# Norms as columns of tokens, regrouped dense pieces in the heads, and a last attention that starts among its gate units

## The chip, the core and the metric

The kernel runs on one core of a Trainium2 chip. The metric is the device time of one execution in microseconds (us); lower is better. The core has five engines that matter here: TensorE (PE, with its weight loads shown as PEld), VectorE (DVE), ScalarE (ACT), GpSimd (POOL) and SyncE (SP, which issues most of the DMAs). Each engine works off its own queue in order, and they wait for each other by semaphores.

## What is computed

Two transformer blocks follow each other on 512 tokens of 1024 features (the second also has 256 context tokens). All is fp32 in and out.

```python
# first block
u = rms_norm(h, norm_mix_pre)
q, k, v ..., gate_a, gate_b = split(u @ w_in)
o_a = nsa_attention(...)            # compressed, selected and window keys, 8 heads
o_b = swa_sink_attention(...)       # window of 128, a sink per head, 8 heads
y = sigmoid(gate_a) * (o_a @ w_up_nsa) + sigmoid(gate_b) * (o_b @ w_up_swa)
h = h + rms_norm(y @ w_out, norm_mix_post)
f = square(relu(rms_norm(h, norm_mlp_pre) @ w_mlp_in)) @ w_mlp_out
h = h + rms_norm(f, norm_mlp_post)
# second block: layer 0 "A" (differential attention), layer 1 "B" (windowed attention)
for i in range(2):
    shift, scale, gate = split(silu(c) @ w_mod[i] + b_mod[i])     # and the same for the context
    hx = rms_norm(x, g[i]) * (1 + scale) + shift
    hc = rms_norm(ctx, g[i]) * (1 + scale_c) + shift_c
    x = x + gate * (mixer_i(hx, hc) @ w_o[i])
return rms_norm(x, final_g)
```

## The kernel before

**Layout.** Activations lie feature-major: 8 tiles of 128 features (partitions) by 512 tokens, or 768 with the context. A weight "unit" is a 1024x128 block of a matrix. SP loads it into `raw` (four buffers), ACT copies it to a rounded high part `w_h` (`split_high`, line 302), POOL subtracts to get the low part `w_l` (line 890), and PE makes three products for each of the 8 feature tiles: high by high, low by high, high by low (`products`, lines 317 and 321). A product of a unit with 512 tokens is thus 24 matmuls. Activations are split likewise: ACT writes the high tile, DVE the low tile.

**Norms.** Each RMS norm needs, for each token, the sum of squares over 1024 features, which lie on partitions. ACT squares the tiles into `sq` (two buffers), DVE adds most of them into `sqsum`, and PE multiplies with a 128x128 matrix of ones, so that each partition gets the sum of its token: a 128x512 result in PSUM. ACT then makes exp(-0.5 ln(mean + eps)) on 128x512 (`make_rstd`, lines 377 and 379) into the SBUF tile `rstd`, and DVE multiplies tiles by it. The norms are: `nm1` (input), `nm2a` (after w_out), `nm2b` (a sum for the next one), `nm3c` (context), `nm3a` (after the MLP), `nm3b` (before layer A), `nm4` (before layer B) and `nm5` (final).

**The order of the work.** It is written out by hand, engine by engine. The projections of the first block come first, then attention `A1` with the gate units woven in, w_up, w_out, and the MLP with 64 units, during which DVE also makes the modulation vectors from `w_mod` (`cps` holds the conditioning products in PSUM banks 4 to 7). Then come layer A's eight heads (`attend`), w_ao (its last feature tile apart, in `last_out`), the 20 units of layer B, attention `A2` of 16 steps, w_bo, and the final norm.

**Heads of layer A.** In `attend` PE alternates between the attention of one head (scores, `turns` that transpose probabilities, value products) and "dense" pieces of the next head's projections. A piece is one of the 8 feature tiles of a unit (6 matmuls of 512 and 256 tokens), and a head has 4 units (q, k, v, g), 32 pieces. A unit writes banks 0 and 1, and the next unit can start only when ACT has copied them out (`take`). The last head has no successor; its dense pieces are seven tiles of each of the eight w_ao units (`partial_out`, 56 pieces), whose results ACT copies to `ao_t` (`take_out`). The rotation of the next head's q and k (`rotate`) stands in DVE's queue at the fourth and fifth query tile.

**Layer B.** The units are 8 of q, 2 of k, 2 of v and 8 gates. The context tiles of the normed input are needed from unit 8 on; DVE and ACT make one of them in each of the units 0 to 7, beside the rotation of that unit's q. Behind unit 13 PE transposes v in two sets through banks 4 and 5. When all 20 units are done, a barrier (`end_phase("bqkv")`) stands ahead of `attn_pe`, `attn_act` and `attn_dve`. A step of `A2` has four rows of scores (two banks each, two slots), minima by DVE (line 615), exponentials by ACT (line 580), scaling by DVE (line 650), transposes by PE (line 516), a copy of each transposed block by ACT (line 564), and value products (line 527).

Of the kernel before, what the change touches and what calls it, by code (L numbers as in the profile page):

```python
# [11 lines left out]
P = 128  # L12
# [58 lines left out]
def build(nc, t, out):  # L71
# [3 lines left out]
    with ExitStack() as ctx:  # L75
# [53 lines left out]
        tick = sm(3)  # L129
        mulx = sm(32).rearrange("p (l v k) -> p l v k", l=2, v=2)  # L130
# [57 lines left out]
        epsh = at("epsh", z + 64, [P, S])  # L188
        varf = at("varf", z + 66, [P, S])
# [70 lines left out]
        PHASES = ["prep", "wout", "heads", "ao", "bqkv"]  # L260
# [76 lines left out]
        NORM_SEMS = ["src", "sq", "add", "mm", "ln", "r", "t", "hi", "lo"]  # L337

        class Norm:
# [4 lines left out]
            def __init__(self, **counts):  # L344
                self.base = dict(Norm.ends)
                for n in NORM_SEMS:
                    Norm.ends[n] += counts.get(n, 1 if n in ("mm", "ln", "r") else 8)
                self.src, self.sq, self.add, self.mm, self.ln, self.r, self.t, self.hi, self.lo = \
                    [Norm.sems[n] for n in NORM_SEMS]

# [30 lines left out]

        none = dict(src=0, t=0, hi=0, lo=0)
        nm1 = Norm(src=0, t=0)
        nm2a = Norm(**none, sq=0, add=KT + 1)
        nm2b = Norm(t=0, ln=0, r=0)
# [3 lines left out]
        nm4 = Norm(src=0, add=4)  # L389
        nm4c = Norm(src=0, sq=0, add=0, mm=0, ln=0, r=0)  # L390
        sq_odd = sem("sq_odd")
        nm5 = Norm(src=0, add=KT - 1, t=FIN, hi=0, lo=0)
# [71 lines left out]
        class Attn:  # L464
            def __init__(self, name, steps, slots, width, sbuf, ptbuf, sbn, finish):
# [9 lines left out]
                self.between_pe = self.between_act = self.between_dve = lambda eng, x: None  # L475
# [67 lines left out]
        def attn_pe(pe, A):  # L543
            attn_scores(pe, A, 0)
            attn_scores(pe, A, 1)
# [4 lines left out]
        def attn_act(act, A):  # L550
            def turned(n):
                st = A.steps[n]
                for b, (o, w) in enumerate(st["blocks"]):
                    x = A.blk[n] + b
                    act.wait_ge(A.t, x + 1)

                    if x >= 4:
                        need = x - 3
                        gd = sum(1 for s in range(len(A.steps)) if A.steps[s]["last"] and A.blk[s + 1] <= need)
                        if gd:  # L560
                            act.wait_ge(A.o, gd)
                        if need - gd:
                            act.wait_ge(A.k, need - gd)
                    nc.scalar.activation(A.pt[0:w, x % 4], ps[0:w, 4 + x % A.tb], ACT.Copy).then_inc(A.te, 1)
                    A.between_act(act, x)

            def finished(n):
                if A.steps[n]["last"]:
                    A.finish["act"](act, A, n, A.grp[n])

            for n, st in enumerate(A.steps):
                for r in range(REP):
                    m = n * REP + r
                    act.wait_ge(A.m, m + 1)
                    if st["sink"] is not None or st["clamp"]:
                        act.wait_ge(A.m, (n + 1) * REP)
                        act.wait_ge(mfix[A], fixn(A, n) + 1)
                    buf = A.sb[n % A.sbn][:, r, 0:st["keys"]]
                    c = (n % 2) * REP + r
                    nc.scalar.activation(buf, buf, ACT.Exp, bias=negm[:, c:c + 1], scale=-1.0,  # L580
                                         accum_out=sums[:, c:c + 1]).then_inc(A.e, 1)
                if st["sink"] is not None:
                    c = (n % 2) * REP
                    nc.scalar.activation(esk[:, c:c + REP], esk[:, c:c + REP], ACT.Exp).then_inc(A.e, 1)
# [1628 lines left out]
```

## Time and profile before

| what | value |
|---|---|
| median of 3 runs | 1720.45 us (1716.83 to 1722.75) |
| the profiled execution's own time | 1721.67 us |
| its span, first to last instruction | 1719.6 us |
| PE busy | 1588.1 us, 92% |
| PE weight loads busy | 1192.6 us, 69% |
| DVE busy | 936.6 us, 54% |
| ACT busy | 764.2 us, 44% |
| POOL busy | 494.5 us, 29% |
| mean granted clock of PE | 0.975 of full |

A busy share is the time in which an engine has an instruction in work, over the span. Weight loads overlap matmuls. The chain of work that ended last runs through PE for 73% of the span, through DVE for 14% and ACT for 6%. Times below are us from the span's start, and a number in brackets is the idle time of the engine ahead of the instruction, with what ended it.

### The profile page before, as it was taken

Reading aid. Unit: us, or ns where it says so; the run is one execution under the profiler, and the core shown is the slowest. Engines: PE = TensorE matmul, PEld = TensorE weight load, DVE = VectorE, ACT = ScalarE, POOL = GpSimd, SP = SyncE. Lnnn points to the kernel's source line nnn. Section 1 sums busy time; section 2 is a strip of 40 time slices with the busy share of each in tenths; the row PEclk is TensorE's granted clock in tenths of the full one; section 3 lists DMA queues with packets and bytes.
Section 4 is the critical chain, followed back from the end, with each engine's and each line's share of the span. In section 5 each row is a group of like instructions: output and inputs, shape, how many; then the busy total and the mean of one; then the engine's idle time right before and its main releaser. Section 6 shows DMA issues by size and latency. Waiting matters only on the chain.

```text
span 1719.6 us, 22679 instructions
## 1 busy us (share of the span) xinstructions
PE 1588.1 (92%) x7940; PEld 1192.6 (69%) x7940; DVE 936.6 (54%) x2204; ACT 764.2 (44%) x1411; POOL 494.5 (29%) x220
## 2 busy tenths in 40 slices
PE   7998999999899999998999999999989697979897
PEld 5885666677688888885777777677667477745455
DVE  7136555283788767556556444644471593156642
ACT  6227766524333222345335443554443531246653
POOL 4542232344244444442211111111224242310012
PEclk9999999999899999999999999999999899979999
DMA  6851112363466665431101111111111131210001
GB/s 193 175 140 45 61 57 73 115 224 115 146 196 193 197 188 195 156 98 62 50 31 44 38 37 37 37 37 37 37 38 50 37 90 59 77 34 1 1 13 62
DMA packets 48397, 149.28 MB, mean 87 GB/s; under 512 B 5782, under 2 KB 9110, under 8 KB 48184
## 3 DMA queue, kind: packets, MB, share of 16 engines
q1 hardware_dynamic: 37080, 112.45, 21.7%
q10 hardware_dynamic: 11232, 35.72, 6.4%
q8 instruction: 51, 0.84, 0.2%
q14 instruction: 34, 0.28, 0.1%
HBM read 141.53 MB, written 6.62 MB: 86 GB/s over the span
## 4 chain that ended last, share of the span: by engine, by line
PE 73%; DVE 14%; ACT 6%; issue 4%; DMA 1%; POOL 0%; ACTq 0%; DVEq 0%; SPq 0%
PE ps L317 37%; PE ps L321 18%; PE ps L497 3%; PE ps L1192 3%; PE ps L516 3%; PE ps L527 3%; PE ps L1228 2%; DVE b_sb L615 1%; DVE x2l L1806 1%; ACT sb L580 1%; DVE xn L1800 1%; PE ps L1204 1%; PE ps L971 1%; DVE ropea L1932 1%; ACT w_h L302 1%
## 5 line engine op out<-in xcount | busy, mean ns | idle before, releaser
L890 POOL TENSOR_TENSOR w_l<-raw,w_h 128x1024 fp32r<-128x1024 f32 (+1 forms) x190 | 457.1, 2406 | 993.8 <-ACT w_h L302 993.8
L302 ACT ACTIVATE w_h<-raw 128x1024 fp32r<-128x1024 f32 x190 | 200.8, 1058 | 396.6 <-PE ps L317 330.6
L317 PE MATMUL ps<-x2h,w_h 128*128 128x512 f32 (+1 forms) x816 | 248.5, 370 | 46.1 <-DVE x2l L1806 22.6
L317 PE MATMUL ps<-x1h,w_h 128*128 128x512 f32 x584 | 239.0, 409 | 19.9 <-POOL w_l L890 10.3
L317 PE MATMUL ps<-x2h,w_l 128*128 128x512 f32 (+1 forms) x816 | 232.0, 350 | 0.0
L321 PE MATMUL ps<-x2l,w_h 128*128 128x512 f32 (+1 forms) x816 | 231.8, 349 | 0.0
L317 PE MATMUL ps<-x1h,w_l 128*128 128x512 f32 x584 | 231.4, 396 | 0.0
L321 PE MATMUL ps<-x1l,w_h 128*128 128x512 f32 x584 | 230.8, 395 | 0.0
L317 PEld LDWEIGHTS ps<-x2h,w_h 128*128 128x128 f32 x816 | 132.3, 190 | 95.1 <-issue 56.1
L317 PEld LDWEIGHTS ps<-x2h,w_l 128*128 128x128 f32 x816 | 132.1, 191 | 20.7
L321 PEld LDWEIGHTS ps<-x2l,w_h 128*128 128x128 f32 x816 | 132.4, 191 | 19.9 <-issue 0.2
L317 PEld LDWEIGHTS ps<-x1h,w_h 128*128 128x128 f32 x584 | 111.8, 191 | 46.1 <-issue 10.4
L317 PEld LDWEIGHTS ps<-x1h,w_l 128*128 128x128 f32 x584 | 111.6, 191 | 24.4
L321 PEld LDWEIGHTS ps<-x1l,w_h 128*128 128x128 f32 x584 | 112.0, 192 | 20.6 <-issue 0.2
L1865 DVE CUSTOM_DVE_ANT_0 terms<-mraw,ps 128x1024 f32<-128x1024 f32 x96 | 116.8, 1217 | 2.5
L1982 DVE CUSTOM_DVE_ANT_0 a_p<-ps,small 128x768 f32<-128x768 f32 (+1 forms) x96 | 71.3, 776 | 68.8 <-issue 68.8
L317 PE MATMUL ps<-m_h,w_h 128*128 128x512 f32 x256 | 99.6, 389 | 0.0
L321 PE MATMUL ps<-m_l,w_h 128*128 128x512 f32 x256 | 99.6, 389 | 0.0
L317 PE MATMUL ps<-m_h,w_l 128*128 128x512 f32 x256 | 99.6, 389 | 0.0
L1490 ACT ACTIVATE a_p<-a_p,small 128x768 f32<-128x768 f32 (+1 forms) x96 | 75.1, 785 | 24.4 <-DVE small L1982 24.4
L615 DVE CUSTOM_DVE_ANT_0 b_sb<-ps,bm 128x512 f32<-128x512 f32 (+1 forms) x64 | 45.9, 755 | 40.0 <-PE ps L497 39.9
L897 POOL TENSOR_TENSOR g_stage<-g_stage,rstd 128x512 f32<-128x512 f32 x16 | 20.5, 1281 | 148.9 <-ACT g_stage L784 148.9
(310 smaller groups left out, 2490.6 us busy)
## 6 DMA issues: line engine op xcount, KB each, us to landing
raw<-in_w_mlp SPq DMA_DIRECT2D x64, 512.0 KB, 4.2
mraw<-in_w_mod ACTq DMA_DIRECT2D x51, 512.0 KB, 3.8
raw<-in_w_a SPq DMA_DIRECT2D x32, 512.0 KB, 3.5
raw<-in_w_att SPq DMA_DIRECT2D x25, 512.0 KB, 11.2
raw<-in_w_b SPq DMA_DIRECT2D x20, 512.0 KB, 3.5
raw<-in_w_g SPq DMA_DIRECT2D x16, 512.0 KB, 3.6
raw<-in_w_ao SPq DMA_DIRECT2D x9, 512.0 KB, 3.5
gates<-g_stage ACTq DMA_DIRECT2D x16, 256.0 KB, 2.1
```

Source lines behind the costliest of these rows:

```text
L302: nc.scalar.activation(split(u)[0], raw[:, u % RAW], ACT.Copy).then_inc(w_hi, 1)
L317: mm = nc.tensor.matmul(o, w[:, k], xh(k), start=(first and k == k0 and wi == 0), stop=(last and k == k1 - 1 and wi == 1))
L321: mm = nc.tensor.matmul(o, w[:, k], xl(k), start=False, stop=False)
L497: mm = nc.tensor.matmul(A.sbank(m + h)[:, o:o + rhs.shape[-1]], st["q"](r + h), rhs, start=st["kstart"][c], stop=True, skip_group_check=True)
L516: mm = nc.tensor.transpose(ps[0:w, 4 + x % A.tb, y * P:(y + 1) * P], A.sb[n % A.sbn][:, r, o:o + w], ident[:])
L527: mm = nc.tensor.matmul(ps[h * HD:(h + 1) * HD, 6 + g % 2, cols], st["v"](h)[b], A.pt[0:w, x % 4, h * 2 * P:(h + 1) * 2 * P], start=(st["f ...
L615: nc.vector.tensor_tensor_reduce(out=A.sb[n % A.sbn][:, r, 0:st["keys"]], in0=A.sbank(m)[:, st["off"]:st["off"] + st["keys"]], in1=st["bia ...
L890: nc.gpsimd.tensor_tensor(l[:, ks], raw[:, u % RAW, ks], h[:, ks].bitcast(F32), ALU.subtract).then_inc(w_lo, 1)
L1192: mm = nc.tensor.matmul(pair(1 + 2 * m)[:, o:o + n], aq[ms, qt * P:(qt + 1) * P], ak[ms, key:key + n], start=True, stop=True)
L1490: nc.scalar.activation(buf, buf, ACT.Exp, bias=negm[:, cc:cc + 1], scale=-1.0, accum_out=sums[:, cc:cc + 1]).then_inc(ha["e"], 1)
L1865: nc.vector.tensor_tensor_reduce(out=terms[:], in0=mraw[:, c % MRAW].rearrange("p k m -> p (k m)"), in1=cps[:, w, :], scale=0.5, scalar=0. ...
L1982: nc.vector.tensor_tensor_reduce(out=a_p[qt % 3][m][:, 0:n], in0=pair(1 + 2 * m)[:, 0:n], in1=zero.to_broadcast([P, n]), scale=1.0, scalar ...
```

## The change

It has three parts, named in its title.

**Norms.** For `nm2a`, `nm2b`, `nm3c`, `nm3a`, `nm3b`, `nm4` and `nm5` the sum of squares is made with the squares as the stationary operand and one column of ones as the moving one, so that a block of 128 tokens gives one column: 128x4 for 512 tokens, 128x6 for 768 (`column_sums`). ACT takes a square root of that (`root`), DVE a reciprocal (`invert`), and PE spreads each column over 128 partitions by a matmul of the broadcast column with the identity (`spread`), into a PSUM bank that DVE's multiplications then read in place of `rstd`. A tiny Sqrt activation stands some time ahead of three of the norms. The final norm is spread twice, and ACT copies one of these for POOL's two tiles. `nm1` and the norm inside the heads stay as they were.

```diff
+        def column_sums(src, bank, n, first, last):
+            for b in range(n // P):
+                mm = nc.tensor.matmul(ps[:, bank, b:b + 1], src[:, b * P:(b + 1) * P], ones[:, 0:1],
+                                      start=(first and b == 0), stop=(last and b == n // P - 1))
+            return mm
+        def root(act, nm, bank, n):
+            nm.wait(act, "mm", 1)
+            nc.scalar.activation(dev[:, 0:n // P], ps[:, bank, 0:n // P], ACT.Sqrt, bias=eps_t[:], scale=1.0 / D).then_inc(nm.ln, 1)
+        def invert(v, nm, n):
+            nm.wait(v, "ln", 1)
+            nc.vector.reciprocal(rcol[:, 0:n // P], dev[:, 0:n // P]).then_inc(nm.rc, 1)
+        def spread(bank, b0, b1):
+            for b in range(b0, b1):
+                mm = nc.tensor.matmul(ps[:, bank, (b - b0) * P:(b - b0 + 1) * P], rcol[:, b:b + 1].to_broadcast([P, P]), ident[:],
+                                      start=True, stop=True)
+            return mm
...
             nm3a.wait(pe, "sq", KT)
-            nc.tensor.matmul(ps[:, 4], ones[:], sq[:, 1, 0:S], start=False, stop=True).then_inc(nm3a.mm, 1)
+            column_sums(sq[:, 1], 4, S, False, True).then_inc(nm3a.mm, 1)
+            nm3a.wait(pe, "rc", 1)
+            nm3c.wait(pe, "lo", KT)
+            spread(5, 0, 4).then_inc(nm3a.r, 1)
```

In `last_out` the squares of every tile go to PE two tiles later, and DVE no longer adds any of them:

```diff
-                    if m >= 2 and m % 2 == 0:
-                        nm4.wait(pe, "sq", m)
-                        sum_part(sq[:, 1], m == 2, False).then_inc(sq_odd, 1)
-                nm4.wait(pe, "add", N_OUT // 2)
-                sum_part(sqsum, False, False)
+                    if m >= 2:
+                        nm4.wait(pe, "sq", m - 1)
+                        column_sums(sq[:, m % 2], 6, SC, m == 2, False).then_inc(sq_sum, 1)
+                nm4.wait(pe, "sq", N_OUT - 1)
+                column_sums(sq[:, 0], 6, SC, False, False)
                 nm4.wait(pe, "sq", N_OUT)
-                sum_part(sq[:, 1], False, True).then_inc(nm4.mm, 1)
+                column_sums(sq[:, 1], 6, SC, False, True).then_inc(nm4.mm, 1)
+                nm4.wait(pe, "rc", 1)
+                spread(7, 0, 4).then_inc(nm4.r, 1)
+                spread(5, 4, 6).then_inc(nm4c.r, 1)
```

Behind the w_out norm DVE's three operations per tile are reordered so that the first low tile comes one operation earlier, and the conditioning products `cps` are cut in two: one half inside the w_out units, one behind the last low tile.

**Heads.** The sizes of the dense pieces change, and DVE's rotations of the next head's q and k come behind the loop over query tiles:

```diff
                 scores(1)
-                dense(4 if more else 3)
+                dense(4)
...
                 turns(4)
-                dense(2 if more else 4)
+                dense(4)
...
-                dense(2 if more else 3)
+                if not more:
+                    dense(3)
                 turns(5)
-                dense(2 if more else 1)
+                if more:
+                    dense(4)
...
-                dense(6 if more else 7)
+                dense(4 if more else 7)
...
-                    if qt in (3, 4) and more:
-                        rotate((i, c + 1), qt - 3, "qk"[qt - 3])
+                if more:
+                    rotate((i, c + 1), 0, "q")
+                    rotate((i, c + 1), 1, "k")
```

**Layer B.** The context tiles are made two per unit in units 0 to 3. The second set of v transposes uses banks 6 and 7. The last gates write banks 6 and 7 (`gate_bank`), the barrier ahead of `A2` is gone, and the scores of the steps 0 and 1 stand between the halves of the last two gate units. ACT and DVE have the parts of these steps between their parts of the gates, and in every step of `A2` ACT copies the first two transposed blocks of the step before among its four exponentials:

```diff
+            pe.wait_ge(hb["free"], 16)
+            for n, u in enumerate((N_B - 2, N_B - 1)):
+                attn_scores(pe, A2, n, (0, 1))
+                split_ready(pe, U_B + u)
+                pe.wait_ge(hb["free"], u - 1)
+                products(U_B + u, b_parts(u), 0, KT // 2, last=False)
+                attn_scores(pe, A2, n, (2, 3))
+                products(U_B + u, b_parts(u), KT // 2, KT, first=False).then_inc(unit, 1)
...
+            for u in range(N_B - 2):
+                take_b(u)
+            attn_exps(act, A2, 0)
+            take_b(N_B - 2)
...
+                act.wait_ge(A.m, m + 1)
+                if n and A.slots == 2 and r >= 2:
+                    attn_turned(act, A, n - 1, (r - 2,))
...
+            attn_minima(v, A2, 0, (0, 1))
+            gate_b(N_B - 3)
+            attn_minima(v, A2, 0, (2, 3))
+            attn_minima(v, A2, 1, (0, 1))
+            gate_b(N_B - 2)
+            attn_scale(v, A2, 0)
+            attn_minima(v, A2, 1, (2, 3))
```

The gate of unit 19 is taken behind step 1 on ACT and DVE. `A1` keeps its order.

## Rows read from the trace of the kernel before

**Rows 1.** The page: its first line, and two groups of its fifth section.

```profile
span 1719.6 us, 22679 instructions
...
L890 POOL TENSOR_TENSOR w_l<-raw,w_h 128x1024 fp32r<-128x1024 f32 (+1 forms) x190 | 457.1, 2406 | 993.8 <-ACT w_h L302 993.8
...
L615 DVE CUSTOM_DVE_ANT_0 b_sb<-ps,bm 128x512 f32<-128x512 f32 (+1 forms) x64 | 45.9, 755 | 40.0 <-PE ps L497 39.9
```

**Rows 2.** Waits of PE: line, whom for, us in total, times, longest.

```profile
PE ps L317 <- DVE x2l L1806: 22.6, 7, 8.6
PE ps L497 <- DVE small L615: 16.1, 19, 1.6
...
PE ps L317 <- ACT ao_t L1478: 6.5, 6, 1.2
PE ps L317 <- ACT a_vT L1459: 5.4, 7, 0.8
PE ps L1204 <- DVE a_p L1997: 5.2, 7, 0.8
```

**Rows 3.** Busy time by window: stretch, length, engines, granted clock, DMA.

```profile
1427.00:1433.00 6.00, 5.63 (x24) 4.89 (x25) 0.22 (x1) 0.00 (x0) 0.00 (x0) 0.70 0.00 0
```

**Rows 4.** Nearest prices: timeline, then lines of PEld and of DVE.

```profile
181.27 0.63 PE L497 MATMUL ps<-kcmp,q_n 64*128 64x32 f32 x8
...
1538.18 1.09 PE L516 MATMUL ps<-ident,b_sb 128*128 128x128 f32 x8
...
L497 PEld LDWEIGHTS ps<-kcmp,q_n 64*128 64x128 f32 x64 | 4.5, 193 | 3.2 <-issue 2.7 <-DVE small L615 0.4
...
L643 DVE RECIPROCAL small<-small 128x4 f32<-128x4 f32 x48 | 8.6, 180 | 1.6
```

**Rows 5.** Timeline of PE, ACT and DVE at the w_out norm.

```profile
426.40 1.12 PE L1034 MATMUL ps<-sq,ones 128*128 128x512 f32 x2 [0.85 <-ACT sq L1357]
...
428.85 1.28 ACT L379 ACT_TABLE_LOAD   x1
...
431.11 1.42 DVE L1780 SCALAR_TENSOR_TENSOR f_t<-f_t,small,rstd 128x512 f32<-128x512 f32 x2 [0.46 <-DVEq L265]
```

**Rows 6.** Timeline of PE and DVE at the two norms behind the MLP.

```profile
794.23 1.12 PE L1070 MATMUL ps<-sq,ones 128*128 128x512 f32 x2 [0.72 <-ACT sq L357]
...
802.90 9.57 PE L1088 MATMUL ps<-sq,ones 128*128 128x512 f32 x16 [1.79 <-ACT sq L1430]
...
800.17 1.42 DVE L1896 SCALAR_TENSOR_TENSOR f_t<-f_t,small,rstd 128x512 f32<-128x512 f32 x2 [4.00 <-ACT rstd L1425]
...
815.17 1.41 DVE L1800 SCALAR_TENSOR_TENSOR xn<-hc,small,rstd 128x512 f32<-128x512 f32 x2 [4.80 <-ACT rstd L1434]
```

**Rows 7.** Timeline of PE in the heads: a value product, eight score instructions.

```profile
1112.60 5.31 PE L1228 MATMUL ps<-a_pt,a_v 128*128 128x512 f32 x12
...
1274.22 1.56 PE L1192 MATMUL ps<-a_k,a_q 64*128 64x512 f32 x8
```

**Rows 8.** Timeline of PE and DVE around the end of w_ao.

```profile
1349.51 1.13 PE L1143 MATMUL ps<-sq,ones 128*128 128x512 f32 x2 [1.05 <-ACT sq L1557]
...
1354.22 1.13 PE L1143 MATMUL ps<-sq,ones 128*128 128x512 f32 x2 [1.07 <-ACT sq L1557]
...
1358.92 2.07 PE L1143 MATMUL ps<-sqsum,ones 128*128 128x512 f32 x2 [2.10 <-DVE sqsum L2049]
...
1367.97 1.41 DVE L1800 SCALAR_TENSOR_TENSOR xn<-hc,small,rstd 128x512 f32<-128x512 f32 x2 [9.10 <-ACT rstd L379]
```

**Rows 9.** Timeline of PE at the waits inside the b units.

```profile
1427.37 0.98 PE L317 MATMUL ps<-x2h,w_h 128*128 128x512 f32 x2 [8.62 <-DVE x2l L1806]
...
1476.60 0.87 PE L1269 MATMUL ps<-ident,b_vT 128*128 128x128 f32 x6 [2.65 <-DVE b_v L2079]
```

**Rows 10.** Timeline of ACT and PE where the last attention starts.

```profile
1499.39 1.06 ACT L302 ACTIVATE w_h<-raw 128x1024 fp32r<-128x1024 f32 x1 [3.90 <-PE ps L317]
...
1529.08 1.97 PE L516 MATMUL ps<-ident,b_sb 128*128 128x128 f32 x8
```

More of the change, by code:

```diff
@@ L548, in attn_pe, with attn_turned @@
                 attn_out(pe, A, n)
[L550 to L565, printed above, removed]
+        def attn_turned(act, A, n, bs):
+            st = A.steps[n]
+            for b in bs:
+                o, w = st["blocks"][b]
+                x = A.blk[n] + b
+                act.wait_ge(A.t, x + 1)
+                if x >= 4:
+                    need = x - 3
+                    gd = sum(1 for s in range(len(A.steps)) if A.steps[s]["last"] and A.blk[s + 1] <= need)
+                    if gd:
+                        act.wait_ge(A.o, gd)
+                    if need - gd:
+                        act.wait_ge(A.k, need - gd)
+                nc.scalar.activation(A.pt[0:w, x % 4], ps[0:w, 4 + x % A.tb], ACT.Copy).then_inc(A.te, 1)
+                A.between_act(act, x)
@@ L569, in finished @@
                     A.finish["act"](act, A, n, A.grp[n])
[L571 to L584, printed above, removed]
-                else:
-                    act.wait_ge(A.e, 5 * n + 4)
-                    nc.scalar.activation(spare, eps_t[:], ACT.Copy).then_inc(A.e, 1)
+            for n in range(n0, len(A.steps)):
+                attn_exps(act, A, n)
                 if n:
-                    turned(n - 1)
+                    attn_turned(act, A, n - 1, range(2 if A.slots == 2 else 0, len(A.steps[n - 1]["blocks"])))
                 if n >= 2:
                     finished(n - 2)
-            turned(len(A.steps) - 1)
+                A.after_act(act, n)
+            attn_turned(act, A, len(A.steps) - 1, range(len(A.steps[-1]["blocks"])))
             finished(len(A.steps) - 2)
@@ L1087, in _ @@
                 nm3b.wait(pe, "sq", k + 1)
-                mm = nc.tensor.matmul(ps[:, 6], ones[:], sq[:, k % 2, 0:S], start=(k == 0), stop=(k == KT - 1))
-                mm.then_inc(n3_sum, 1)
+                column_sums(sq[:, k % 2], 6, S, k == 0, k == KT - 1).then_inc(n3_sum, 1)
+            nm3b.wait(pe, "rc", 1)
+            spread(7, 0, 4).then_inc(nm3b.r, 1)
             for k in range(KT + LAG):
@@ L1139, in partial_out @@
                         mm.then_inc(unit, 1)
-            def sum_part(src, first, last):
-                nc.tensor.matmul(ps[:, 6, :], ones[:], src[:, 0:S], start=first, stop=last)
-                return nc.tensor.matmul(ps[:, 7, 0:C], ones[:], src[:, S:SC], start=first, stop=last)
             def last_out():
@@ L1285, in _ @@
             nm5.wait(pe, "add", KT - 1)
[L1286 removed]
+            column_sums(sqsum, 4, S, True, False)
             nm5.wait(pe, "sq", KT)
[L1288 removed]
+            column_sums(sq[:, 1], 4, S, False, True).then_inc(nm5.mm, 1)
+            nm5.wait(pe, "rc", 1)
+            spread(5, 0, 4).then_inc(nm5.r, 1)
+            spread(6, 0, 4).then_inc(nm5.r, 1)
         @block.scalar
@@ L1422, in _ @@
             act.wait_ge(varf_ok, 1)
-            nc.scalar.activation(rstd[:, 0:S], varf[:], ACT.Ln).then_inc(nm3a.ln, 1)
-            nm3a.wait(act, "ln", 1)
-            nc.scalar.activation(rstd[:, 0:S], rstd[:, 0:S], ACT.Exp, scale=-0.5).then_inc(nm3a.r, 1)
+            nc.scalar.activation(dev[:, 0:4], varc, ACT.Sqrt).then_inc(nm3a.ln, 1)
             for k in range(KT):
```

347 lines of the change are left out of this document (198 added, 149 removed).

## The prediction

> **What bounds the kernel now.** I began with the page: a span of 1719.6 us [rows 1]. The execution it shows took 1721.67 us, so 2.1 us lie around the span, and it is 1.2 us above the median of 1720.45. TensorE (PE) is busy over nine tenths of the span, so only what PE waits for, what it does at half clock, or work taken from it can shorten the kernel. The second view was who keeps PE waiting [rows 2]: low tiles of normed activations, the minima of the attentions, and evacuations that come when PE has just finished a unit and wants its bank back. I then read the timeline where the diff touches these waits. PE also pays after long gaps: after the 8.62 us gap at 1418.75 the clock stood at 0.70 on average over 6 us, a mix of 1.2 and 2.4 GHz [rows 3].
>
> **Prices.** The column sums and the spreads do not exist before. A column sum of 512 tokens is 4 fp32 matmuls with one moving column, 8 pairs of weight load and matmul. The nearest row is 8 pairs with 32 moving columns: 0.63 us in all. I take 0.63 (0.95 for the 12 pairs of 768 tokens), and near twice that where the clock is halved; above, 8 loads that overlap nothing, at 0.19 each, are 1.5. A spread of 4 blocks is 8 pairs with 128 columns, which is what 8 transposing pairs cost: 1.09 us. A spread at 1.2 GHz would cost what the first such step does, 1.97. A reciprocal on 128x4 is 0.18 us, and I take the same for a 128x4 activation [rows 4, 10]. I allow 0.1 us for each hand-over.
>
> What the old chain holds is seen behind the w_out product [rows 5]: from the last ones-matmul (426.40) to the first user (431.11) 4.7 us, with Ln, Exp and a 1.28 us table load ahead of each. The new chain is sum 0.63, root 0.3, reciprocal 0.3, spread 1.3, hand-over and barrier 0.4, so 2.9 to 3.0: it saves 1.7 (0.8 with the halved clock, 2.0 above). Here the root's table is loaded under the w_out products, where ScalarE has room; half of the conditioning products go there too, and the other half behind the last low tile, where they delay ScalarE's first split of the MLP by nothing that I can see (its cover gone, at most 0.5).
>
> ScalarE's table loads were weighed against the skill. The trace loads a table for Ln and again for Exp, 1.28 us each. The Trainium skill (ScalarE: Activation LUTs, Table sets: the hidden batching unit) says Ln and then Exp need one load, and Exp and then Sqrt two; by that rule the old norm would be a load cheaper than the trace shows, and this edit would save 1.3 us less per norm. The trace disagrees, and the sum goes by it.
>
> **Part by part.**
> 1. w_out norm: 1.7, as above.
> 2. The two norms behind the MLP [rows 6]. The first chain ran from 794.23 to 800.17. Now it is 2.8 us and ends near 797.0, but PE waits for it, and the 6.3 us of context products that it did meanwhile (to 801.11, the end before the 1.79 us wait) now run to 803.3. The sums of squares then start later than before (802.90), but they no longer trail: a square of 0.63 us and a column sum of 0.5 alternate in two buffers at 0.65 us per tile, and end near 808.5 in place of 812.47. The second chain takes 1.9 in place of 2.7 us. Gain 4.3 (3.0 halved, 5.0 if sums cost nothing).
> 3. Seven head turns with a successor. Two waits stand in each [rows 2]: 0.74 us for a combined probability tile, since VectorE rotates the next q before it, and 0.77 for the evacuation of v, since PE reaches the end of that unit just then. The rotations now come after the last tile, where VectorE is idle; and the end of the v unit falls ahead of the value product, 5.3 us [rows 7]. Both waits go, 1.5 x 7 = 10.5. It costs nothing while those covers hold; if others surface, half, 5; 11.5 above.
> 4. The last head. Six waits of 1.1 us for ao_t [rows 2] are each at a unit's end inside a dense piece. Pieces now end with the unit, so scores (1.56 us for eight instructions, half for four) or turns stand there [rows 7]. The first gains nothing, because the seventh product must now wait for its low tile ahead of the scores; the next four give 1.2, 0.6, 0.6 and 0.6. Gain 3 (1.5 to 4.5).
> 5. The w_ao tail and its norm [rows 8]. Two tiles take 4.7 us from sum to sum, with a 1.05 us wait for a fresh square. With sums two tiles late nobody waits, and PE needs 2 x 1.1 for products (4.7 less the wait and 1.3 of sums) and 2 x 0.65 for sums, 3.5; over three and a half pairs 4.2. From the last product (1356.82) to the first user (1367.97) it was 11.15 us. Now: 2.1 for update, split and square as before, 0.65 sum, 0.3 root, 0.3 reciprocal, 12 spread pairs 1.7, barrier 0.4, so 5.5. Together 9.9; this stretch is sparse and may run at half clock, so I take 9 (7 to 10.5).
> 6. The eighth b unit [rows 9]. PE waits 8.62 us for the eighth context tile, which VectorE makes one per unit. At two per unit all eight are there after four units, some 15 us before they are wanted. 8.62 goes, and so does the slow clock behind it (6 us at 0.70, 1.8): 10.4 (8.6 to 10.8). The second set of v transposes has its own banks: 2.65 goes (2.0 to 2.7).
> 7. The start of the last attention [rows 10]. From the end of unit 17 (1499.39) to the first transposes (1529.08) it is 29.7 us: 10.9 of two units, then scores and softmax alone, at half clock. Now the scores lie among the units. PE's work is 10.9 + 5 x 1.1 = 16.4, but VectorE's chain is longer: four minima at 0.75 each [rows 1], four exponentials about as long, the gate of unit 18 (queued behind them on ScalarE with its 1.06 us split), scaling behind GpSimd's 2.4 us low tile [rows 1], and two more minima before the third step's scores. Walked through, transposes start 19.1 us after unit 17. Gain 10.6. Later the gate of unit 19 and its split sit between exponentials (-1.5), and the second step is at full clock (+1.4). I take 10.5 (7 to 13). Queued behind gate 18 on VectorE are the scale of step 0 and half the minima of step 1; PE waits for these with its second half unit as cover.
> 8. ScalarE copies turned blocks between exponentials. In most steps PE waits for minima and not for these, so they buy little: 2 over 16 steps (0 to 4).
> 9. The end. Norm chain 1.7 shorter for VectorE's six outputs, but GpSimd's two get theirs from a second spread and a copy, 0.8 earlier; the last transfer leaves some 1.3 earlier (0.7 to 1.75). The chain's old parts are those of part 1 [rows 5].
>
> Sum: 1.7 + 4.3 + 10.5 + 3 + 9 + 10.4 + 2.65 + 10.5 + 2 + 1.3 = 55.4. From 1721.7 that is 1666; I say 1666 us for the median.
>
> **Rivals.**
> - Weight loads pace the column sums. For: each load is shown with 0.19 us. Against: 8 pairs in 0.63 [rows 4] means that they overlap. If nothing did, a tile of part 5 would take 3.4 us, and the eight sums of part 2 12 us: together some 20 us back, 1686. The Trainium skill (TensorE: Matmul & The Clock Gate, LDWEIGHTS (loading the stationary operand)) gives columns / 1.2 ns, 107 ns for each of these loads; by that 12 pairs are 1.3 us, parts 2 and 5 lose about 7 us, and the time is 1673. The trace disagrees where 8 loads of 128 columns fit into 0.63. A mechanism of this kernel with that price, 1673 to 1686, gets 0.08.
> - The early attention does not pay: the chain over gate 18 is as long as the old idle time, or the gates' splits collide with every step. Then part 7 is 3 and not 10.5, 1674. For: two engines' queues are threaded through each other, and GpSimd's low tile holds up VectorE's scaling. 0.17.
> - The heads stay at their period, since VectorE's and ScalarE's chain and not PE's is the pace: part 3 gives 0 to 3, 1675. Against: in a turn only these two waits are above 0.4 us, and PE is busy in nearly all the rest. 0.09.
> - The table of the root lacks a function used between roots, so that it is loaded again in each norm: 5 x 1.28 back, 1672. For it speaks only that Ln and Exp did so. 0.06.
> - The other side: in the last attention the third and fourth exponential now wait for transposes of the step before, which wait for scaled probabilities. If that closes a circle, each of 16 steps (9.1 us for the first, from 1529.08 to 1538.18 [rows 4, 10]) grows. From 3.5 us per step on the kernel is slower: 1730 at 4 us. Against: transposes of two blocks are there when two exponentials are done. 0.02.
> - The change does little, since other waits take over in most places: 1710 to 1722, 0.03.
>
> **How the numbers follow.** The forecast of 1666 has a chance of 0.55. Its terms' lower ends add up to 39, their upper ends to 65, but they seldom fall together. The range runs from 1656 to 1682 and takes in the single rivals at 1672 to 1675. Within 0.3% (about what a measurement of this kernel can tell from no change) lies almost nothing: faster 0.95, same 0.02, slower 0.03.
>
> **What would show it.** Right: no wait of PE for x2l longer than about 4 us behind the w_ao norm, none near the eighth b unit; 8 column pairs near 0.6 us; one table load or none per norm, outside the chain; no wait of PE for a_vT or a_p above 0.5 us in the heads, so that a turn is 1.5 us shorter; 19 us from unit 17 to the first transposes of the last attention. Wrong: PE waits for VectorE's minima among the last units, table loads right ahead of roots, column sums above 1 us, steps of the last attention longer than now, or new waits at the unit boundaries of the heads.

## The result and the profile after

The changed kernel takes 1689.98 us (median of four, 1689.45 to 1696.08) against 1719.94 for the kernel before: a ratio of 0.9834, with a 95% interval of 0.9806 to 0.9863. It is 30 us faster. The forecast was 1666 us, 54 faster by the same median, with a range that ended at 1682. So the sign was right, the size was a little over half, and the time lies outside the range.

The page of the changed kernel, its first line and the two groups that answer to [rows 1]:

```profile
span 1688.6 us, 23139 instructions
...
L928 POOL TENSOR_TENSOR w_l<-raw,w_h 128x1024 fp32r<-128x1024 f32 (+1 forms) x190 | 454.8, 2395 | 970.5 <-ACT w_h L304 970.5
...
L640 DVE CUSTOM_DVE_ANT_0 b_sb<-ps,bm 128x512 f32<-128x512 f32 (+1 forms) x64 | 45.9, 755 | 37.4 <-PE ps L521 37.2
```

The waits of PE, which answer to [rows 2]:

```profile
PE ps L521 <- DVE small L640: 11.6, 17, 1.5
...
PE ps L319 <- DVE x2l L1897: 8.5, 10, 2.6
PE ps L319 <- DVE x1l L1868: 6.4, 7, 3.5
...
PE ps L319 <- DVE a_g L2035: 2.9, 1, 2.9
...
PE ps L319 <- ACT ao_t L1537: 2.2, 3, 1.0
```

By this view the change did nearly all that it should: the waits for x2l in the norms of layers A and B fell from 22.6 to 8.5 us, those for a_vT and for a_p have left the list, ao_t has 2.2 in place of 6.5. By the two pages PE is idle for 82.9 us of the span and not 131.5 (span less busy time). That is 48.6 us less waiting for a span that is 31.0 us shorter: PE is also busy for longer, 1605.7 us and not 1588.1. Cutting both spans at the same events shows where. All rows are lengths in us, of which the column "after, less before" adds up to the 31.0 us between the spans; e2 is an experiment below.

| stretch (ends at) | before | after | after, less before | forecast | e2, less before |
|---|---|---|---|---|---|
| start to PE's wait for w_out's last square | 425.55 | 425.08 | -0.5 | 0 | -0.4 |
| w_out norm and MLP (wait for its last square) | 367.97 | 369.31 | +1.3 | -1.7 | +1.5 |
| two norms (first a product with x2l) | 24.00 | 27.46 | +3.5 | -4.3 | -1.4 |
| first a units, seven turns (last head's scores) | 426.16 | 415.71 | -10.5 | -10.5 | -12.5 |
| last head (wait for the last ao_t) | 95.31 | 90.84 | -4.5 | -3.0 | -4.7 |
| last pass of w_ao (its last product) | 17.83 | 24.50 | +6.7 | -9.0 with the next | -0.6 |
| norm of w_ao (first b product) | 13.59 | 13.57 | 0.0 | | -4.9 |
| b units (end of unit 17) | 128.98 | 117.08 | -11.9 | -13.05 | -11.9 |
| start of the last attention (first transposes) | 29.69 | 17.84 | -11.9 | -10.5 with the second step | -11.8 |
| its steps and the last product | 176.51 | 173.16 | -3.4 | -2.0 | -3.4 |
| end | 14.01 | 14.05 | 0.0 | -1.3 | +0.8 |

Everything that moves work between other work came out near its forecast, from 1.1 us less (the b units) to 1.5 us more. Everything that has to do with a norm did not: 11.5 us are lost in the four rows from the w_out norm to that of w_ao (without the heads), where 15.0 of gain were forecast, and the end gives nothing for 1.3. The seven turns hit 10.5 partly by luck, as is told below. The timeline of PE in the changed kernel, at the norms behind the MLP and in the last pass of w_ao, which answers to [rows 6, 8]:

```profile
793.44 0.95 PE L387 MATMUL ps<-ones,sqsum 128*128 128x1 f32 x8
...
805.37 11.45 PE L387 MATMUL ps<-ones,sq 128*128 128x1 f32 x64
...
1333.42 1.39 PE L387 MATMUL ps<-ones,sq 128*128 128x1 f32 x12
...
1347.58 0.84 PE L1200 MATMUL ps<-x2h,w_l 128*128 128x512 f32 x2
1348.22 2.55 PE L387 MATMUL ps<-ones,sq 128*128 128x1 f32 x12
...
1352.70 7.67 PE L387 MATMUL ps<-ones,sq 128*128 128x1 f32 x36
1360.95 2.93 PE L402 MATMUL ps<-ident,small 128*128 128x128 f32 x12 [0.58 <-DVE small L397]
```

Two things are to be seen. A column sum of 8 pairs takes 0.95 us and one of 12 takes 1.39, not 0.63 and 0.95. And a few microseconds later the same sum takes 2.55, and even the products beside it take 0.84, where the same two products took 0.51 in the kernel before:

```profile
1356.31 0.51 PE L1156 MATMUL ps<-x2h,w_l 128*128 128x512 f32 x2
```

The windows of the changed kernel say why; the column behind POOL's is the granted clock:

```profile
803.00:806.00 3.00, 3.00 (x29) 3.00 (x27) 3.00 (x6) 0.00 (x0) 0.00 (x0) 1.00 0.02 5
806.00:809.00 3.00, 3.00 (x23) 3.00 (x24) 2.91 (x5) 1.88 (x3) 0.00 (x0) 0.81 0.00 0
809.00:815.00 6.00, 6.00 (x30) 6.00 (x30) 0.00 (x0) 1.91 (x4) 0.00 (x0) 0.50 0.00 0
...
1333.00:1336.00 3.00, 3.00 (x25) 2.83 (x23) 1.42 (x3) 1.79 (x3) 0.76 (x1) 1.00 0.37 66
1336.00:1342.00 6.00, 6.00 (x30) 5.71 (x31) 2.28 (x4) 0.94 (x2) 0.00 (x0) 0.58 0.13 55
1342.00:1348.00 6.00, 6.00 (x23) 5.43 (x23) 1.14 (x2) 1.60 (x2) 0.00 (x0) 0.50 0.00 0
```

PE is shown as busy all the time, 6.00 of 6.00 us, and its clock is nevertheless granted at 0.50, that is 1.2 in place of 2.4 GHz. It was doing one-column sums just before: weight loads with one column streamed behind each. In the kernel before, where PE was less busy, the clock was at 1.00 in the same stretches:

```profile
809.00:815.00 6.00, 3.19 (x7) 0.97 (x6) 1.37 (x3) 5.17 (x7) 0.00 (x0) 1.00 0.00 0
1342.00:1348.00 6.00, 5.18 (x25) 3.68 (x24) 4.41 (x8) 2.54 (x3) 2.37 (x2) 1.00 0.29 87
```

At 0.50 a tile of the last pass takes 4.48 us (1343.74 to 1348.22 from sum to sum), where the prediction had 3.5 us for two.

A last surprise stands at head 0. The Sqrt table is in ScalarE when the gate's Tanh comes:

```profile
855.75 1.28 ACT L1520 ACT_TABLE_LOAD   x1
857.04 0.81 ACT L1520 ACTIVATE a_g<-ps 128x768 f32<-128x768 f32 x1
```

PE waits 2.94 us for a_g there (at 858.98), and 1.51 in the kernel before, which loads no table ahead of this gate:

```profile
853.26 0.59 PE L317 MATMUL ps<-x2h,w_h 128*128 128x512 f32 x2 [1.51 <-DVE a_g L1940]
```

### The profile page after: what moved, and what is told of

Same layout as the page of the kernel before. It is cut to its first block, busy times and chain, and to the rows that moved or that the text cites. A ratio compares the mean times of both kernels' runs of the same rounds, so it can differ in the third digit from the quotient of the medians.

```text
span 1688.6 us, 23139 instructions
## 1 busy us (share of the span) xinstructions
PE 1605.7 (95%) x8164; PEld 1229.9 (73%) x8164; DVE 936.9 (55%) x2206; ACT 750.5 (44%) x1401; POOL 491.7 (29%) x220
## 4 chain that ended last, share of the span: by engine, by line
PE 81%; DVE 9%; ACT 5%; issue 4%; POOL 1%; DMA 0%; PEldq 0%; ACTq 0%; POOLq 0%; PEld 0%; DVEq 0%
PE ps L319 41%; PE ps L323 20%; PE ps L521 3%; PE ps L1239 3%; PE ps L540 3%; PE ps L551 3%; PE ps L1275 2%; PE ps L387 2%; DVE b_sb L640 2%; PE ps L1251 1%; PE ps L1009 1%; ACT sb L601 1%; DVE tg L1824 1%; ACT w_h L304 1%; DVE b_sb L675 1%
## 5 line engine op out<-in xcount | busy, mean ns | idle before, releaser
L319 PE MATMUL ps<-x1h,w_h 128*128 128x512 f32 x584 | 239.9, 411 | 17.2 <-POOL w_l L928 10.4
```

The lines of the kernel that those rows point to most:

```text
L319: mm = nc.tensor.matmul(o, w[:, k], xh(k), start=(first and k == k0 and wi == 0), stop=(last and k == k1 - 1 and wi == 1))
```

## Experiments

My theory after this comparison (A): the one-column sums cost both by themselves and by the clock that they bring down. The main rival (B): the new chain of root, reciprocal and spread, with its hand-overs over three engines, costs more than Ln and Exp did.

**e1: the squares of w_ao added on VectorE.** Two column sums in place of eight.

```diff
-                    if m >= 2:
-                        nm4.wait(pe, "sq", m - 1)
-                        column_sums(sq[:, m % 2], 6, SC, m == 2, False).then_inc(sq_sum, 1)
-                nm4.wait(pe, "sq", N_OUT - 1)
-                column_sums(sq[:, 0], 6, SC, False, False)
+                nm4.wait(pe, "add", N_OUT - 1)
+                column_sums(sqsum, 6, SC, True, False)
...
+                if m:
+                    add_square(v, nm4, m - 1, SC)
```

> The changed kernel, but in the last pass of w_ao VectorE adds up the squares (128x768 adds, about 0.95 us each by the trace of before) and TensorE makes two column sums at the end and not eight. Theory A (the one-column sums are what costs: eight of them at 1.4 to 2.55 us, and they drag the granted clock of their stretch to 0.50): a tile then takes VectorE's 1.14 + 0.95 = 2.1 us in place of 4.48, and from the last wait for ao_t (1329.74 in the changed kernel) to the first b products it is 27 to 29 us and not 36.7; 8 to 9.5 us faster than the changed kernel, 1681 to 1682. Theory B (the chain behind the sums, root, reciprocal and spread over three engines, is what costs): the chain is untouched, so under 3 us are gained, 1687 to 1690.

Measured: 1682.57 us. From 1329.37 to the first b product at 1356.73 it is 27.4 us, 9.4 less than in the changed kernel, as A had it; the median is 7.4 less. But the clock still fell, this time where PE waited for an add. Timeline and windows of e1:

```profile
1345.36 2.72 PE L387 MATMUL ps<-ones,sqsum 128*128 128x1 f32 x12 [3.39 <-DVE sqsum L367]
...
1335.00:1341.00 6.00, 4.20 (x19) 2.93 (x20) 6.00 (x10) 2.79 (x4) 0.00 (x0) 1.00 0.19 73
...
1344.00:1350.00 6.00, 4.64 (x22) 4.64 (x22) 1.31 (x3) 1.19 (x2) 3.09 (x1) 0.50 0.21 55
```

**e2: 64 columns in place of one.** The same sums, and 63 columns of each block that nobody reads.

```diff
-                mm = nc.tensor.matmul(ps[:, bank, b:b + 1], src[:, b * P:(b + 1) * P], ones[:, 0:1],
+                mm = nc.tensor.matmul(ps[:, bank, b * 64:(b + 1) * 64], src[:, b * P:(b + 1) * P], ones[:, 0:64],
...
-            nc.scalar.activation(dev[:, 0:n // P], ps[:, bank, 0:n // P], ACT.Sqrt, ...
+            nc.scalar.activation(dev[:, 0:n // P], ps[:, bank, 0:n // P * 64:64], ACT.Sqrt, ...
```

> The changed kernel, but each column sum moves 64 columns of ones per block and not one, so TensorE streams 64 times the columns behind the same weight loads; the extra columns are not read. Theory A1 (what halves the clock is that TensorE hardly streams columns while it makes these sums): the granted clock of the last pass of w_ao and of the sums behind the MLP stays near 1.00, a sum of 768 tokens stays near 1.4 us, and 8 to 14 us come back, 1676 to 1682. Theory A2 (weight loads alone set the pace and the clock has another cause, such as the waits of the stretch): the clock falls as before and the time is 1689 to 1695, a little more for the columns.

Measured: 1671.53 us (ratio to the kernel before 0.9716, 0.969 to 0.9741), 18.5 us faster than the changed kernel by an edit that only adds work to PE, and more than the 8 to 14 us that I expected. Timeline and windows of e2 at the same two places:

```profile
805.55 7.55 PE L387 MATMUL ps<-ones,sq 128*128 128x64 f32 x64
...
1333.76 1.45 PE L387 MATMUL ps<-ones,sq 128*128 128x64 f32 x12
...
1338.56 4.13 PE L387 MATMUL ps<-ones,sq 128*128 128x64 f32 x36
1343.27 1.60 PE L402 MATMUL ps<-ident,small 128*128 128x128 f32 x12 [0.58 <-DVE small L397]
...
809.00:815.00 6.00, 5.26 (x43) 4.89 (x42) 0.32 (x3) 2.32 (x5) 0.00 (x0) 1.00 0.00 0
...
1335.00:1341.00 6.00, 6.00 (x49) 5.73 (x48) 2.39 (x5) 3.59 (x4) 1.02 (x1) 1.00 0.01 3
```

Twelve pairs take 1.45 us with 64 columns and 1.39 with one: at full clock the columns are nearly free. The clock stays at 1.00 in these two stretches, so the 36 last pairs take 4.13 and not 7.67 us and the spread 1.60 and not 2.93. This settles A's second half, since the edit changes nothing there but how many columns PE streams. It is not a lucky execution either: in all eight traced kernels with 64 columns and eight sums (e2 and e5 to e11) the last pass of w_ao takes 17.1 to 17.2 us and the norm behind it 8.7, and with one column the same pass takes 24.5 in the changed kernel and 17.8 in e3, and the norm 13.6 in both. Of the 18.3 us between the two spans 17.0 lie in the two norms, the last pass and its norm; most of the rest is in the seven turns (2.0), where the clock is at 0.50 from 859 to 862.5 behind the wait for a_g in the changed kernel, and at 1.00 behind the same wait in e2.

**e3: the sums behind the MLP among context products.** `first_ctx(1)` is cut into pieces that stand behind the single sums.

```diff
-            first_ctx(1)
             for k in range(KT):
                 nm3b.wait(pe, "sq", k + 1)
                 column_sums(sq[:, k % 2], 6, S, k == 0, k == KT - 1).then_inc(n3_sum, 1)
+                if k < KT - 1:
+                    first_ctx(1, k, k + 1 if k < KT - 2 else KT)
```

> The changed kernel, but behind the MLP the eight column sums of the second norm stand between the products of the second context unit and not behind both. Theory A (few columns, low clock, and a chain that starts too late): the sums run at full clock at 0.95 to 1.05 us, the last ends near 813 and not 816.8, the spread takes 1.1 and not 2.1 us; 4 to 5 us faster than the changed kernel, 1685 to 1686. Rival (the squares' own pace, one in 1.26 us from VectorE, is the bound): about 1 us, 1689.

Measured: 1683.87 us (1681.73 to 1690.74), which looks like a hit and isn't one. In its own stretch (from 794.41 to 820.48) it gained 0.6 us, because the clock fell there all the same, to 0.73 at 806 and 0.50 from 809 on. Another 6.7 us are in the last pass of w_ao, which the edit does not touch: there the clock held until 1343.3 and not until 1337, although e3 was only 1.4 us ahead, so that three more sums ran at 1.40 us. Windows of e3:

```profile
809.00:815.00 6.00, 6.00 (x30) 6.00 (x29) 0.00 (x0) 0.63 (x1) 0.00 (x0) 0.50 0.00 0
1335.00:1341.00 6.00, 6.00 (x47) 5.67 (x47) 3.04 (x6) 1.99 (x3) 0.00 (x0) 1.00 0.05 20
...
1344.00:1350.00 6.00, 6.00 (x30) 5.90 (x29) 1.14 (x2) 1.90 (x2) 2.35 (x1) 0.50 0.10 10
```

The place where the clock gives way is not fixed in such a stretch; a total of a few microseconds less proves nothing about an edit without its window.

**e4: the second norm behind the MLP and that of w_ao wholly as before**, in the changed kernel: `column_sums` there replaced by the ones-matmuls into 128x512 (and 128x256), VectorE's adds of every other square, `make_rstd` in place of `root`, `invert` and `spread`.

> The changed kernel with the second norm behind the MLP and the norm of w_ao wholly as before: wide ones-matmuls, pairs of squares added on VectorE, Ln and Exp with two table loads each. By the stages of the two traces these norms cost 3.5 and 6.6 us more than before, so theory A gives 1690 - 10 = 1680 us, and another 1.4 less where the Exp table is there again for the gate of head 0 (1678.6). The rival, that the new norms gain as forecast and the loss comes from elsewhere (clock or buffers of the stages ahead), gives over 1692.

Measured: 1674.62 us. Undoing what the change's title begins with makes the kernel 15 us faster, 5 more than the stages gave, since the clock that stays at 1.00 (0.50 only from 1346 on, in the wait behind the last sums) helps the neighbours too. From the end of the last sum of w_ao's norm to the first b product it is 5.69 us in e4, 6.10 in the changed kernel and 4.75 in e2. So the new chain is 0.9 us shorter than the old one at full clock, and 0.4 longer at half clock, where its spread takes 2.93 us and not 1.60. B is wrong: what the chain costs too much is again the clock. Against e2, which keeps it, e4 is 3.1 us slower, although it has no Tanh table to load at head 0.

The next six runs stand on e2, whose clock is steady in the two stretches of sums.

**e5 and e6: the two edits of the heads.** e5 puts VectorE's two rotations back between the combinations; e6 puts back TensorE's pieces.

```diff
e5
                         mins(qt + 2)
-                if more:
-                    rotate((i, c + 1), 0, "q")
-                    rotate((i, c + 1), 1, "k")
+                    if qt in (3, 4) and more:
+                        rotate((i, c + 1), qt - 3, "qk"[qt - 3])
e6
-                dense(4)
+                dense(2 if more else 4)
...
-                dense(4 if more else 7)
+                dense(6 if more else 7)
```

> The kernel of e2 (64-column sums, 1671.5 us, granted clock steady in the two norm stretches), with VectorE's rotations of the next q and k back between the combinations of the probability tiles, as before the change. If the rotations are what made TensorE wait 0.74 us for a combined tile in each turn, the seven turns are 0.74 us longer each: 5.2 us, 1676.7. Rival (TensorE's new pieces alone would have removed that wait): within 1 us of e2.

> The kernel of e2 with TensorE's dense pieces in the heads and in the last head cut as before the change (two and six tiles around the value products, not four and four; three and one in the last head). By the trace the wait of 0.77 us for a_vT returns in seven turns, 5.4 us, and the waits for ao_t in the last head, about 3 (forecast) to 4.5 us (measured): 1679.9 to 1681.4 in all. Rival (the pieces do nothing once the rotations are moved): within 1 us of e2 but for the last head, 1674.

Measured: 1677.98 and 1681.71 us, 6.4 and 10.2 us over e2. The waits of PE, of e5 and then of e6:

```profile
PE ps L1251 <- DVE a_p L2092: 5.2, 7, 0.9
```

```profile
PE ps L319 <- ACT ao_t L1535: 6.5, 6, 1.2
PE ps L319 <- ACT a_vT L1516: 5.4, 7, 0.8
```

Each part of the change removes exactly the wait that it was said to, and each alone leaves the other. A turn is 55.00 us in e5, 55.07 in e6, 54.01 in e2 (54.08 in the changed kernel) and 55.97 before. Undoing them costs 0.99 and 1.06, about the whole 1.96, and more than the 0.74 and 0.77 of the waits; where the other 0.5 us of a turn come from is not shown. The last head is 93.72 us in e6 and 90.62 in e2, so the pieces are worth 3.1 there.

**e7: ScalarE's copies of turned blocks behind all four exponentials.**

```diff
-                if n and A.slots == 2 and r >= 2:
-                    attn_turned(act, A, n - 1, (r - 2,))
```

> The kernel of e2 with ScalarE's copies of turned blocks in the last attention again behind all four exponentials of the next step. Forecast in the prediction: 2 us over 16 steps (0 to 4), so 1673.5 (1671.5 to 1675.5). Rival: they pace the steps, and more than 4 us come back, over 1675.5.

Measured: 1675.68 us, 4.2 over e2. Its trace is 2.5 us longer from the last attention's third step to the last product, with waits of PE for b_pt of 3.4 us in nine places where e2 has 1.0 in two. The trace agrees with the forecast of 2 within its range, while the medians' 4.2 lie just above it, on the side of the rival; whether the other 1.7 us are more than the spread of the runs (1674.69 to 1676.54, and 1667.46 to 1672.49 for e2) stays open.

**e8: the last attention begun behind the last gate.** Units 18 and 19 go back into the loop of units, and scores, exponentials and minima of step 0 and 1 behind it; the gates keep their new banks, and no barrier is put back.

> The kernel of e2 with the last attention begun behind the last gate and not among the gates, its copies still between exponentials; gates keep their own banks. The traces give 11.85 us from the end of unit 17 to the first transposes (forecast 10.5), so 1682 to 1684. Rival (the early start only moves a wait, since the steps are paced by VectorE and ScalarE): under 6 us, below 1677.5.

Measured: 1682.39 us (1677.93 to 1687.46), 10.9 over e2. In the trace it is 11.0 us more from the first b product to the first transposes and nothing in the steps behind them (173.18 us and 173.16), so the rival of a wait that is only moved is out. PE waits again for the gate and for each pair of minima:

```profile
PE ps L521 <- DVE small L640: 16.4, 20, 1.6
...
PE ps L521 <- DVE b_g L2139: 2.4, 1, 2.4
```

**e9: the Tanh table ahead.** One activation of one column right behind the root, while ScalarE waits for the spread.

```diff
             nc.scalar.activation(dev[:, 0:4], ps[:, 6, 0:256:64], ACT.Sqrt, ...).then_inc(nm3b.ln, 1)
+            nc.scalar.activation(dev[:, 6:7], eps_t, ACT.Tanh)
```

> The kernel of e2 with one more activation: a Tanh of one column right behind the root of the second norm behind the MLP, so that its table is loaded while ScalarE waits for the spread. If the load of 1.28 us ahead of head 0's gate is what lengthened TensorE's wait for a_g from 1.51 to 2.94 us, the wait is 1.5 us again and 1.4 us come back, 1670.1. Rival (the gate is late for another reason, or the table is put out again before the gate): the wait stays at 2.9 us, 1671.5.

Measured: 1669.8 us (1668.85 to 1672.66), 1.7 under e2; by the total alone it can't be told from e2. In the trace the load stands right behind the root (811.44), and PE's wait is what it was before the change:

```profile
PE ps L319 <- DVE a_g L2036: 1.5, 1, 1.5
```

**e10: VectorE's order behind the w_out norm as before.** A low tile two tiles behind its scale.

```diff
-            for k in range(KT):
-                if k >= 1 and k + 1 < KT:
-                    f_scale(k + 1)
-                if k + 1 < KT and k >= 1:
-                    f_add(k + 1)
-                f_low(k)
...
+            for k in range(KT + 2):
+                if k < KT:
+                    f_scale(k)
+                if 1 <= k <= KT:
+                    f_add(k - 1)
+                if k >= 2:
+                    f_low(k - 2)
```

> The kernel of e2 with VectorE's order behind the w_out norm as before the change (a scale, an add and a low tile two tiles apart). Theory: VectorE is the pace from the first low tile to the eighth, 2.05 us a tile in the new order, because each low tile waits for ScalarE's split of the same tile, and 1.93 in the old; the new order has its first low tile a step earlier (about 1.3 us) and loses it again over eight tiles. So the first tile comes 1.2 us later and the eighth 0.5 to 1 us earlier, and the time is 1670.5 to 1671.5. Rival: TensorE at half clock is the pace, and the later start costs 1 us, 1672.5.

Measured: 1671.1 us; by the total it can't be told from e2. The trace tells it. The first low tile comes at 432.71 (e2: 431.45), most tiles are 1.92 us apart (e2: 2.05), and the seventh starts at 443.59 (e2: 444.34), although e10 is 0.3 us later at its first scale. Not all of these 2.0 us is the distance of the tiles: the new order also has 2.66 us between its first two, and the old one only 1.26 between its sixth and seventh, when no scale is left. And the 0.13 us a tile are no wait for ScalarE's split, which my expectation named as the cause: VectorE goes from a scale to the add behind it in 0.78 us in e2, where that add needs this scale, and in 0.65 in e10. From the wait for w_out's last square to that for the MLP's it is 367.5 us, 1.9 less than in e2 and 0.5 less than before the change. Timeline of PE in e10:

```profile
433.60 0.77 PE L319 MATMUL ps<-x1h,w_h 128*128 128x512 f32 x1 [4.42 <-DVE x1l L1868]
```

**e11: e2 with the edits of e9 and e10.**

> The kernel of e2 with the edits of e9 and e10 together: if they add, 2 us less than e2, 1669.5.

Measured: 1668.63 us (1667.36 to 1668.88), ratio 0.97 (0.9682 to 0.9718), 21 us faster than the changed kernel and the lowest median of all runs, though its 2.9 us under e2 are within the spread of e2's runs (1667.46 to 1672.49).

**e12: e11, with every other square of w_ao added on VectorE**, so that six sums of 64 columns are left.

> The kernel of e11, and in the last pass of w_ao VectorE adds every other square (as before the change), so TensorE makes six 64-column sums and not eight: per two tiles TensorE has 2.2 us of products and 1.45 of sum, 3.65 and not 4.8. The last product comes 3.3 us earlier, but the last sums wait 2.1 us for an add, as in the trace of before. Net 1 to 2 us less than e11, 1667.5 to 1668.5, as long as the granted clock stays at 1.00. If the clock falls in the sparser stretch the sums cost 2.5 us and the kernel is slower than e11, 1671 or more.

Measured: 1671.85 us (1671.39 to 1673.39), 3.2 over e11: the expectation's second branch. Two sums fewer, and from the first product of the last pass (1317.94) to the first b product it takes 5.7 us longer than in e11. Timeline and windows of e12:

```profile
1336.68 2.82 PE L387 MATMUL ps<-ones,sqsum 128*128 128x64 f32 x12 [2.10 <-DVE sqsum L2144]
...
1332.00:1335.00 3.00, 2.57 (x18) 2.15 (x18) 1.28 (x3) 1.15 (x2) 0.00 (x0) 1.00 0.00 0
1335.00:1338.00 3.00, 1.32 (x6) 1.33 (x7) 1.62 (x3) 1.59 (x2) 2.17 (x1) 0.70 0.00 0
1338.00:1344.00 6.00, 5.42 (x26) 5.23 (x26) 0.19 (x1) 0.27 (x1) 0.83 (x1) 0.50 0.29 87
```

In e11 the clock is at 1.00 from 1326 to 1338. Its extra sums fill PE's waits, and at the end of the stretch that is worth more than what they cost.

## Why the prediction was wrong, step by step

**The price of a column sum** is the step that failed first. I took 0.63 us for 8 pairs, from score instructions with 32 moving columns [rows 4]. Their name shows a stationary operand of 64 rows, 64x128, and in the kernel they alternate between two heads, which lie in the lower and the upper 64 partitions. The row was used for sums of 128 rows as if neither mattered; which of the two makes it cheap no run separates. A row with 128x128 operands stood beside it, 8 transposing pairs in 1.09 us, and I used it for the spreads only. Measured at full clock: 0.95 us for 8 pairs, 1.39 for 12, so 0.12 us a pair. Part 2 even took 0.5 us for its sums of 8 pairs, and part 5 took 0.65 for its own, which have 12 pairs each. I had given "weight loads pace the column sums" 0.08, and argued it away by that same row. The Trainium skill (TensorE: Matmul & The Clock Gate, LDWEIGHTS (loading the stationary operand)) has 107 ns for each load of 128 columns. By that 12 loads are 1.28 us, an estimate; the trace comes near it with 1.39 us for 12 pairs, and what I called the trace's disagreement was my choice of row.

**The clock** is the larger one. Part 5 says "this stretch is sparse and may run at half clock, so I take 9 (7 to 10.5)", and parts 1 and 2 have the halved clock only in a lower end. The clock at 0.50 is no mark-down of a microsecond: it nearly doubles every sum (1.39 to 2.55), slows the products between them (0.51 to 0.84) and doubles the spread (1.60 to 2.93). I had looked for low clock behind gaps, as in [rows 3]. Here PE is shown busy without a gap when the clock falls. e2 puts a number on it: with the clock held in the stretches of sums and nothing else improved, 18.5 of the 24 us that were missing are there. Of my rivals only those in which the change does little or harm lay at 1690 or above. The one that came true, that weight loads pace the sums, was priced without the clock and ended at 1686. The range was also too narrow by its own terms: their lower ends add up to 35.6 us and not to 39, which alone allows 1686.

**Part 1** (1.7, came out as a loss of 1.3): the chain itself gained 1.6, from 4.71 us (426.40 to 431.11) to 3.12 (426.01 to 429.13), and the first low tile reaches PE at 432.29 in place of 435.20. It was given back in part by something that I did not cost at all, the new order of VectorE's three operations a tile. e10 puts 1.9 us on it. Even with the old order only 0.5 of the 1.6 is left at the end of the stretch; where the rest goes stays open.

**Part 2** (4.3, came out as a loss of 3.5): both clock and pair price. In e2 the stretch gains 1.4. Of the 2.9 us that are missing there, 2.4 are the eight sums, 7.55 us where 5.2 were forecast, and 0.8 the context products ahead of them, 7.1 us where 6.3 were: behind the first norm's chain the clock is at 0.50 under them (799 to 801), in e2 as in the changed kernel, and 64 columns did not help there. PE had just waited twice, 0.74 and 0.86 us; in the kernel before it did these products in place of waiting.

**Parts 3 and 4** (10.5 and 3): right in mechanism, 1.89 us a turn for 1.5, 4.5 for the last head. e5 and e6 show that the two waits are separate and add up. That part 3 came out at 10.5 to the tenth is luck: seven turns of 1.89 are 13.2, and 2.7 of it were lost again in the same stretch. Half of that is the Tanh table, 1.4 us at head 0, which part 3 lacks. I had given "the table of the root lacks a function used between roots" 0.06 and priced it inside the norms; the load came outside them, once, in front of a gate. e9 shows it.

**Part 5** (9, came out as a loss of 6.7): as above. With the clock held, in e2, it gains 5.5 (4.9 and 0.6); the rest is about what eight sums of 1.39 us cost over the 0.95 of my price list.

**Part 6** (13.05): 11.9. The eighth tile is in time and the second set of transposes does not wait, as said. The difference lies at the start of the units: from the second low tile on PE now waits 1.7 us in four places and 0.56 once for a weight's low part, where it waited 0.96 in two before (the eighth tile's 8.62 aside).

**Parts 7 and 8** (10.5 and 2): 11.85 and 3.35. Walked through, the start was to take 19.1 us and took 17.84. e8 and e7 give 10.9 and 4.2 when undone, and 11.0 and 2.5 by the trace.

**Part 9** (1.3): nothing. The new chain from the last product to VectorE's first output is 6.07 us where it was 6.10: two sums of 1.05 and 1.03 are as long as the wide ones (1.13 and 1.02), and two spreads, at a falling clock, take 3.56 us together. The price came from part 1, where the old chain took 4.71 us from the last ones-matmul to the first user. Here it took only 3.69 (1708.00 to 1711.69), since the first table load lies under the sums. ACT in the kernel before:

```profile
1707.68 1.28 ACT L1591 ACT_TABLE_LOAD   x1
...
1709.77 1.28 ACT L1593 ACT_TABLE_LOAD   x1
```

The new chain takes 3.71 (1676.91 to 1680.62) and not 3.0. What root and reciprocal save on the one load that is left goes into the spread.

## What to carry to other kernels

A matmul with one moving column cost here what its pair of load and matmul takes, 0.12 us, and a string of them also cost TensorE's clock. When the clock falls in a stretch where the engine looks busy, try more columns in the same instructions (e2) before taking instructions away (e12); products put between the sums did not hold it (e3). Price an instruction by a row whose stationary operand has the same rows and columns and lies in the same partitions, and where the clock may fall price everything in the stretch at both levels, neighbours included. And read a gain of a few microseconds off the stretch that was edited, for the clock can give or take as much elsewhere.

## What was not expected of the hardware

- TensorE at 6.00 us busy of 6.00 by the profile is granted 0.50 of its clock while it runs one-column sums, and 1.00 with the same sums of 64 columns; at full clock these cost 0.06 us more for 12 pairs.
- The point at which the clock falls moves between kernels whose code in that stretch is the same: 1337 in the changed kernel, 1343.3 in e3, which is worth 6.7 us.
- After a Sqrt activation the next Tanh loads its table: one load of 1.28 us at the next gate (855.75), 1.4 us of TensorE's wait.
